# One PSUM operand for the frequent VectorE operations of four attention layers and a hybrid layer

## What is computed

```python
def rope(x, positions):                     # rotation of queries and keys
    return concatenate([x1 * cos - x2 * sin, x2 * cos + x1 * sin])
def dense_causal_attention(q, k, v, block_q):
    s = jnp.where(q_pos >= key_pos, einsum(q, k) * scale, NEG_INF)
    p = jax.nn.softmax(s, axis=-1)
    return einsum(p, v)
def rmsnorm(x, g): return x * rsqrt(mean(x * x) + eps) * g
shift, scale, gate = split(silu(c) @ ada_w[i] + ada_b[i])   # per layer, 1024 x 3072
h = rmsnorm(x, norm_g[i]) * (1 + scale) + shift
```

## Time and profile before

| | |
|---|---|
| runs, us | 3306.7, 3315.63, 3318.36 |
| profiled execution, its own time | 3318.54 us |
| its span | 3316.6 us |
| mean granted TensorE clock | 0.941 |
| TensorE busy | 3015.2 us, 91% |
| VectorE busy | 1104.9 us, 33% |
| ScalarE busy | 648.0 us, 20% |
| GpSimd busy | 883.3 us, 27% |
| stages, us from the start | MLA 113 to 387, SWA to 701, NSA to 1263, MLA to 1557, hybrid attention to 1840, the rest to 3316 |

### The profile page before, as it was taken

How to read it: one execution, slowest core, us unless ns; L and a number is a source line. 1 busy time by engine, 2 the same in 40 slices (tenths; PEclk the granted TensorE clock), 3 DMA queues, 4 the chain that set the end, 5 groups by cost and what they waited for, 6 DMA issues and landing times.

```text
span 3316.6 us, 27803 instructions
## 1 busy us (share of the span) xinstructions
PE 3015.2 (91%) x10138; PEld 1655.1 (50%) x10138; DVE 1104.9 (33%) x2086; ACT 648.0 (20%) x1460; POOL 883.3 (27%) x556
## 2 busy tenths in 40 slices
PE   1799978999999998998788978999999999999997
PEld 1356534556666654564455647444444444444443
DVE  5553365333475544534544245200000221100001
ACT  1123122321323331232133122100000100100000
POOL 4580282038180005703810000183000480000000
PEclk7799989999999998998798988999999999999999
DMA  5441342135141113412310100253222452222222
GB/s 176 138 128 46 95 133 63 40 115 143 39 127 36 29 40 113 126 57 85 111 29 1 51 25 13 84 169 114 76 65 78 134 166 76 63 76 76 68 78 69
DMA packets 267402, 278.05 MB, mean 84 GB/s; under 512 B 39093, under 2 KB 240167, under 8 KB 267175
## 3 DMA queue, kind: packets, MB, share of 16 engines
q1 hardware_dynamic: 239655, 176.04, 17.6%
q0 software_dynamic: 27648, 100.68, 9.8%
HBM read 274.59 MB, written 2.10 MB: 83 GB/s over the span
## 4 chain that ended last, share of the span: by engine, by line
PE 86%; DVE 8%; ACT 2%; DMA 2%; issue 1%; SPq 0%; DVEq 0%; PEld 0%; ACTq 0%; PEldq 0%
PE psum L673 44%; PE psum L815 10%; PE psum L1265 9%; PE psum L1100 3%; PE psum L700 3%; PE psum L789 2%; PE psum L1131 2%; PE psum L717 2%; PE psum L801 2%; PE psum L1086 2%; DVE arena L1914 1%; DVE ada_sum L1858 1%; PE psum L1136 1%; PE psum L937 1%; PE psum L938 1%
## 5 line engine op out<-in xcount | busy, mean ns | idle before, releaser
L673 PE MATMUL psum<-h,ring 128*128 128x512 f32 (+1 forms) x3216 | 1391.8, 593 | 33.0 <-ACT h L1394 29.9
L673 PEld LDWEIGHTS psum<-h,ring 128*128 128x128 f32 x3216 | 617.4, 194 | 769.7 <-issue 753.9
L600 POOL DMA_DIRECT2D ada_ring<-in_ada_w x192 | 113.1, 589 | 1836.3 <-DVE gains L1872 1600.3
L616 POOL TENSOR_TENSOR ada_sum<-ada_sum,ada_ring 128x1024 f32<-128x1024 f32 x168 | 404.2, 2406 | 13.2
L815 PE MATMUL psum<-og,ring 128*128 128x512 f32 x768 | 333.1, 593 | 2.3 <-DVE og L2377 2.0
L612 POOL TENSOR_TENSOR ada_ring<-ada_ring,cond 128x1024 f32<-128x1024 f32 x168 | 320.1, 1905 | 5.3 <-POOL ada_sum L616 1.6
L1265 PE MATMUL psum<-arena,ring 128*128 128x512 f32 x704 | 302.5, 592 | 0.0
L815 PEld LDWEIGHTS psum<-og,ring 128*128 128x128 f32 x768 | 144.6, 190 | 181.8 <-issue 178.3
L2387 DVE TENSOR_TENSOR arena<-psum,arena 128x512 f32 x44 | 30.4, 692 | 573.8 <-PE psum L673 573.8
L1265 PEld LDWEIGHTS psum<-arena,ring 128*128 128x128 f32 x704 | 133.8, 190 | 168.4 <-issue 168.4
L2010 DVE SCALAR_TENSOR_TENSOR x<-psum,mods,x 128x512 f32<-128x512 f32 x64 | 48.1, 751 | 481.3 <-PE psum L1265 272.2
(11 more groups left out here) (266 smaller groups left out, 2846.9 us busy)
## 6 DMA issues: line engine op xcount, KB each, us to landing
ada_ring<-in_ada_w POOLq DMA_DIRECT2D x192, 512.0 KB, 4.1
ring<-in_ffn_w_gate SPq DMA_DIRECT2D x22, 1024.0 KB, 5.3
ring<-in_ffn_w_up SPq DMA_DIRECT2D x22, 1024.0 KB, 5.3
ring<-in_ffn_w_down SPq DMA_DIRECT2D x32, 704.0 KB, 4.6
ring<-in_sc_w_in SPq DMA_DIRECT2D x12, 1024.0 KB, 5.1
ring<-in_mla_w_in SPq DMA_DIRECT2D x10, 1024.0 KB, 5.7
ring<-in_ada_w SPq DMA_DIRECT2D x8, 1024.0 KB, 5.5
ring<-in_mla_w_out SPq DMA_DIRECT2D x8, 1024.0 KB, 5.2
```

The costliest lines, as they stand in the source:

```text
L600: pool.dma_start(ada_ring[:, i % 2, :], w[k * P:(k + 1) * P, first(part)]).then_inc(arrived[i % 2], n.give(f"ada_in{i % 2}", 16))
L616: step = nc.gpsimd.tensor_tensor(total, total, piece, ALU.add)
L673: m = pe.matmul(tile.at[:, part], lhs(k), rhs(k), start=(k == 0), stop=(k == K - 1))
```

## The change

Every VectorE operation that is frequent in the attention layers and read two operands from SBUF, or one in the doubled rate, now reads one operand from PSUM.

- ScalarE writes the exponentials back into the score bank instead of the probs buffer. VectorE's scaling (`normalise`, `weigh`) reads the bank and writes the probs buffer; the three small operations of the compressed branch read the bank too.
- A rotation's `raw * cos` is made when the tile is taken (`take_raw`), from PSUM, beside the copy to `raw`. `rotate` multiplies the turned tile by `sin` in its own bank and adds `tmp0` to it from there. The hybrid layer keeps the old sequence under the name `rotate_normed`.
- The reciprocals of MLA's latents go to the score banks 2 and 3, and the norm reads them there.

```diff
-                        nc.scalar.activation(depth.probs(step)[:, 0:256], depth.bank(step)[:, 0:256], ACT.Exp, scale=SCALE64
+                        nc.scalar.activation(depth.bank(step)[:, 0:256], depth.bank(step)[:, 0:256], ACT.Exp, scale=SCALE64
...
-                        p, source = depth.probs(step)[:, at:at + w], depth.bank(step)
...
-                        e = nc.scalar.activation(p, source, ACT.Exp, bias=neg_max[:, step % 4, g:g + 1], scale=scale,
+                        scored = depth.bank(step) if w > T else depth.bank(step)[:, at:at + w]
+                        e = nc.scalar.activation(scored, scored, ACT.Exp, bias=neg_max[:, step % 4, g:g + 1], scale=scale,
...
+            def take_raw():
+                tile = next_tile()
                 done(tile)
                 if n.of["rope_ready"].at:
                     dve.wait_ge(S["rope_ready"], n.now("rope_ready"))
-                nc.vector.tensor_tensor(tmp[:, 0, 0:width], source, cos, ALU.mult
+                nc.vector.tensor_copy(raw[:, 0, :], tile.at)
+                nc.vector.tensor_tensor(tmp[:, 0, :], tile.at, rope[:, 0, :], ALU.mult).then_inc(tile_used[tile.bank], 1)
+                return tile
+
+            def rotate(dsts, taken):
+                tile = next_tile()
+                done(tile)
+                evacuated(taken)
+                settle(nc.vector.tensor_tensor(tile.at, tile.at, rope[:, 1, :], ALU.mult))
+                for rows_d, dst in dsts:
+                    turned = nc.vector.tensor_tensor(dst, tmp[rows_d, 0, :], tile.at[rows_d, :], ALU.add)
+                turned.then_inc(tile_used[tile.bank], 1)
+                evacuated(tile)
+                dve.sem_inc(S["rope_ready"], n.give("rope_ready"))
...
-                        last = nc.vector.tensor_scalar(p[:, at:at + w], p[:, at:at + w], row_inv[:, b, g:g + 1], None, ALU.mult)
+                            last = nc.vector.tensor_scalar(p[:, at:at + w], scored[:, at:at + w], row_inv[:, b, g:g + 1], None,
+                                                           ALU.mult)
...
-                copy_tile(raw[:, 0, :])
+                taken = [take_raw()]
...
-                    settle(nc.vector.reciprocal(lora_rms[:, i, :], lora_rms[:, i, :]))
+                    settle(nc.vector.reciprocal(SB[i], lora_rms[:, i, :]))
...
-                        last = nc.vector.scalar_tensor_tensor(lora[:, k, :], lora[:, k, :], g, lora_rms[:, i, :],
+                        last = nc.vector.scalar_tensor_tensor(lora[:, k, :], lora[:, k, :], g, SB[i],
...
-                        return nc.vector.tensor_scalar(p[:, 0:w], p[:, 0:w], row_inv[:, b, 0:1],
+                        return nc.vector.tensor_scalar(p[:, 0:w], scored[:, 0:w], row_inv[:, b, 0:1],
```

More of the change, by code:

```diff
@@ L1898, in final_norm @@
                                                    ).then_inc(S["x_normed"], n.give("x_normed"))
-            def rotate(dsts, source, tile, cos=None, sin=None, width=T):
-                cos = rope[:, 0, :] if cos is None else cos
-                sin = rope[:, 1, :] if sin is None else sin
+            def take_raw():
+                tile = next_tile()
                 done(tile)
@@ L1906, in rotate, with rotate_normed @@
                     dve.wait_ge(S["rope_ready"], n.now("rope_ready"))
-                nc.vector.tensor_tensor(tmp[:, 0, 0:width], source, cos, ALU.mult
+                nc.vector.tensor_copy(raw[:, 0, :], tile.at)
[11 more added lines that the diff above has]
+                dve.sem_inc(S["rope_ready"], n.give("rope_ready"))
+            def rotate_normed(dst, source, tile):
+                done(tile)
+                dve.wait_ge(S["rope_ready"], n.now("rope_ready"))
+                nc.vector.tensor_tensor(tmp[:, 0, :], source, C["ax_cos"], ALU.mult
                                         ).then_inc(S["dve_step"], n.give("dve_step"))
-                nc.vector.tensor_tensor(tmp[:, 1, 0:width], tile.at[:, 0:width], sin, ALU.mult
-                                        ).then_inc(tile_used[tile.bank], 1)
+                nc.vector.tensor_tensor(tmp[:, 1, :], tile.at, C["ax_sin"], ALU.mult).then_inc(tile_used[tile.bank], 1)
                 dve.wait_ge(S["dve_step"], n.now("dve_step"))
                 evacuated(tile)
-                for rows_d, dst in dsts:
-                    turned = nc.vector.tensor_tensor(dst, tmp[rows_d, 0, 0:width], tmp[rows_d, 1, 0:width], ALU.add)
-                turned.then_inc(S["rope_ready"], n.give("rope_ready"))
+                nc.vector.tensor_tensor(dst, tmp[:, 0, :], tmp[:, 1, :], ALU.add).then_inc(S["rope_ready"], n.give("rope_ready"))
             every, low, high = slice(0, P), slice(0, 64), slice(64, P)
@@ L1956, in normalise @@
                     G = len(u["groups"])
-                    p = depth.probs(done)
+                    p, scored = depth.probs(done), depth.bank(done)
                     dve.wait_ge(S["exp_done"], n.take("exp_done"))
                     if weigh is not None:
-                        weigh(u, b, p).then_inc(S["probs_ready"], n.give("probs_ready"))
+                        weigh(u, b, p, scored).then_inc(S["probs_ready"], n.give("probs_ready"))
                         return
@@ L2036, in mla @@
                     gate_tile(mla_gate[0][:, e, :], mla_sig[:, e, :], next_tile())
-                rotate([(low, mla_kpe[0:64, 0, :]), (high, mla_kpe[64:P, 1, :])], raw[:, 0, :], next_tile())
+                rotate([(low, mla_kpe[0:64, 0, :]), (high, mla_kpe[64:P, 1, :])], taken[0])
                 def part(name, pair):
@@ L2075, in query @@
                 def query(pair):
-                    copy_tile(raw[:, 0, :])
+                    taken[0] = take_raw()
                 def gate(pair):
@@ L2081, in turn @@
                 def turn(pair):
-                    rotate([(every, swa_q[:, pair % 2, :])], raw[:, 0, :], next_tile())
-                copy_tile(raw[:, 0, :])
+                    rotate([(every, swa_q[:, pair % 2, :])], taken[0])
+                taken = [take_raw()]
                 skip(1)
-                rotate([(low, swa_k[0][0:64, 0, :]), (high, swa_k[1][64:P, 1, :])], raw[:, 0, :], next_tile())
+                rotate([(low, swa_k[0][0:64, 0, :]), (high, swa_k[1][64:P, 1, :])], taken[0])
                 query(0)
@@ L2137, in turn, with weigh @@
                 def turn(pair):
-                    rotate([(every, nsa_q[:, pair % 2, :])], raw[:, 0, :], next_tile())
-                def weigh(u, b, p):
+                    rotate([(every, nsa_q[:, pair % 2, :])], taken[0])
+                def weigh(u, b, p, scored):
                     if u["branch"]:
```

25 lines of the change are left out of this document (13 added, 12 removed).

## The result

The changed kernel takes 3288.37 us, the median of five runs (3271.46, 3273.36, 3288.37, 3289.11, 3289.71); the kernel before, measured beside it, 3310.77 (3303.59 to 3318.36). The ratio of the means is 0.9914, with a 95% interval of 0.9885 to 0.9944: a gain of 28 us, where the medians are 22.4 apart. Six further runs of the changed kernel in a later comparison gave 0.9913 [0.9889, 0.9936]. The forecast was 3280 us, between 3259 and 3302. The time lies inside; the gain behind it, 35.7 us from 3315.6, came out smaller, and the kernel before measured 5 us lower beside the changed one than when the forecast was made.

What follows compares the result with a forecast made beforehand. TensorE's waits on VectorE operations, many stretched by GpSimd, bounded the possible gain at 79.8 us; terms 19.6 + 3 + 9.2 + 2.9 + 3.0 - 2 gave 35.7 us, so 3280 us, range 3259 to 3302.

Steps and rivals of the forecast that it cites:

- SWA openings, 19.6 us: Eight SWA openings: TensorE's waits on the rotation fall from 38.2 to 18.6 us, a gain between 15 and 22.6.
- The clock term of 3 us: SWA: matmuls behind long stands run at a low clock; shorter stands gain 3 us (0 to 8).
- The undisturbed opening, 2.0 us: SWA opening with GpSimd idle: TensorE's wait goes from 2.24 us to 2.0.
- MLA starts, 9.2 us: Two MLA layer starts: TensorE's wait for the rotation's addition shortens by 4.6 us each, 9.2 in all.
- the zero: MLA: copy's bank held 0.68 us longer, set against the shorter rotation behind it: zero (-2 to +1 over both layers).
- NSA, 2.9 and 3.0 us: NSA: start's wait falls from 4.9 to 2.0 us, gaining 2.9; four waits on the scaling go, gaining 3.0.
- The hybrid layer, a loss of 2 us: Hybrid attention: dearer scalings raise waits from 19.0 to 23.9 us; with some 3 back, loss 2 (gain 3 to loss 12.8).
- one collision fewer saves a stretch at lowered clock, which costs some 3: Hybrid layer: avoiding one collision keeps the clock from falling for a stretch, giving back some 3 us.
- Rival 3: Hybrid layer: idle time lowers the clock; ten more slow units cancel the gain, 18 of 32 give 3347 us; chance 0.06.
- Rival 1: SWA: the next wait, such as the sinks' addition meeting GpSimd, takes over; gain 23 us, time 3293; chance 0.14.
- some 17 and some 55: Whole kernel: stated lowest and highest total gain in us from the terms' ends, 3261 to 3299 us.
- The scaling's fixed part: PSUM scalings: by the skill page some 65 ns more each, about 2 us over the hybrid's 32 units; forecast assumed proportional cost.

Runs made afterwards that it cites:

- e5: Kernel before, with GpSimd's conditioning multiply and add narrowed from 1024 columns to 8 (all but each chunk's first multiply): 3251.45 us, ratio 0.9811.
- e6: Changed kernel with GpSimd's conditioning multiply and add narrowed from 1024 columns to 8 (all but each chunk's first multiply): 3255.55 us, ratio 0.9826.
- e4: The changed kernel run again unedited, to see how two executions differ stage by stage: 3284.52 us, ratio 0.9913.
- e1: Kernel before with only the rotations changed; exponentials, scalings and latents as before: 3287.08 us, ratio 0.9928.
- e3: Changed kernel with the hybrid layer's exponentials and scalings back in SBUF: 3280.18 us, ratio 0.9901.
- e2: Kernel before with only the exponentials and scalings moved to PSUM; rotations and latents as before: 3312.91 us, ratio 1.0009.
- e10: Changed kernel with the sinks' addition written as two one-column additions with a scalar operand: 3275.17 us, ratio 0.9888.
- e7: Changed kernel with only the first 5 units of each half of the hybrid's attention keeping exponentials in PSUM: 3274.45 us, ratio 0.9896.
- e12: Changed kernel with split sinks' addition, hybrid norms and rotations also using PSUM, and only 5 units per hybrid half in PSUM: 3268.79 us, ratio 0.9857.

## Why the prediction was right, and where not

The place and the mechanism were right. Operations with two SBUF operands stretch while GpSimd works, one operand in PSUM takes that away, and e5 and e6 show that the whole balance hangs on it. That the total fits is in part luck: the stages that can be read came out 4 us better than their terms, and the gain expected in the other two, NSA and the second MLA, can't be confirmed. By its own terms:

- **SWA openings, 19.6 us.** The waits fell by 18.1 us, in place of eight waits of 4.8 on average eight of 2.5. The term let the sinks' addition collide in three openings at 0.86 us each, 2.6 us in all; in this trace it did in three, which waited 4.8, 3.3 and 2.4 us. Without a meeting they wait 2.8, 1.9 and 1.9 (e6), so it cost some 4 us; in e4 it cost 1.7, in one opening. The clock term of 3 us: TensorE was busy for 268.8 us in place of 274.5 at a clock of 0.96 in place of 0.92, which is 5.7. In e4 the waits fell by 20.3 and the busy time by 3.6. Either way both together are near 23.8, against 22.6 in the sum.
- **The undisturbed opening, 2.0 us**, came as 1.9, in four of the eight; the first opening has 2.0, and the second 2.8 where it meets nothing.
- **MLA starts, 9.2 us.** 14.7 became 5.5: 9.2. The first stage fell by 4.2 to 4.5 us, the expected 4.6. That leaves nothing for the copy's bank, as the zero had it. The second start is in a stage that in one of eight traces was 6 us longer.
- **NSA, 2.9 and 3.0 us.** Both waits fell as said (4.9 to 2.0, and 3.0 to nothing); the stage took 562.2 before, and 558.2 to 559.4 in six of the eight traces with the new code, so it shows some 3 of these 5.9 us, against the one trace before.
- **The hybrid layer, a loss of 2 us.** The waits rose to 26.2 us (23.9 expected), but the layer came out 1.4 us shorter. By 1.4 us alone that would not be firm; the three traces with the old code there (before, e1, e3) and the four with the new (changed, e2, e4, e10) give 588.3 to 590.5 and 586.9 to 588.4. The step that failed is "one collision fewer saves a stretch at lowered clock, which costs some 3". Before, the clock was at its lower level from 1614 to 1655 us and once more from 1672 to 1679; after, only from 1571 to 1594, and that is 9.8 us of TensorE's busy time in the first half (143.2 to 133.4), while its waits for the scaling there did not fall (11.5 to 13.1). The second half's 6.3 us of loss is 16 units at 0.39, as priced.
- **Rival 3** did not happen: once the clock had risen, the second half was granted 1.00 to its end, at 9.5 to 10.3 us busy of 12. Rival 1's mechanism did, in part: the sinks' addition took some 4 us of the openings in one trace and 1.7 in the other, around the 2.6 that the forecast gave it.

**The sum.** In the stages that repeat (the first, SWA, the hybrid) I had expected 4.6 + 22.6 - 2 = 25.2 us; the traces give 4.4 + 23.7 + 1.4 = 29.5, and 1.7 more in the rest, where nothing was changed and which scatters by 3.3. In NSA and the second MLA I had expected another 10.5. The runs give 28 us altogether, with an interval of 18 to 38, so the 35.7 of the sum are not excluded, but the best value leaves nothing for those two stages. The traces say otherwise: in six and seven of eight with the new code they are 3 to 4 and 10.5 to 12 us shorter than in the one trace before. But that one is of an execution 7 us above the mean of its five, and how the kernel before scatters there isn't known. Whether those two stages gained stays open; several profiled executions of the kernel before would be needed.

Two sums in the prediction do not come out. Its terms' own ends add up to a gain of 12.3 and 51.7 us, not "some 17 and some 55", and without a collision the SWA openings would gain 22.2 and not 22.6. The measured gain lies inside either pair of ends.

**The scaling's fixed part, and short idle times.** The Trainium skill, "VectorE: DVE Perf Modes", section "The TRN2 errata", gave a PSUM scaling some 65 ns more than the width does. The widths that stand undisturbed in both kernels don't show it: 343 - 274 = 69 ns at 128 elements and 1018 - 620 = 398 at 768, which is 0.54 and 0.52 ns an element with nothing fixed on top. The Trainium skill, "TensorE: Matmul & The Clock Gate", section "A second HAM failure mode: psum-queue depth-cycling", spoke for rival 3. The traces have such falls of the clock where the units were uneven (e3, e7, and the earlier trace rows) and none for the short, even idle times: in the changed kernel's second half TensorE was busy for 9.5 us of 12 at a granted clock of 1.00.

## What to carry to other kernels

When two engines collide, test it by silencing the other engine before rewriting anything: one small edit to GpSimd here (e5, and e6 beside it) showed the size of the gain and its limit. Protect a chain from its end, the operation that TensorE waits for, since the next unprotected operation meets the collision instead, even one of two elements: e1 protects the end and has nearly all, e2 protects the start and has nothing (a part of e1's gain, up to 8 us in SWA by e5 and e6, is the operation that it moved out of the chain). Where GpSimd is idle the scaling out of PSUM only costs (5.5 to 6 us in the hybrid's second half), so choose such a form by what runs beside it, not by operation.

## What I had not expected of the hardware

- A VectorE operation of 128 x 2 elements, 0.16 us alone, took 2.15 us when it met GpSimd's 128 x 1024 multiplication and 2.25 when it met its addition. The same sum written with a scalar operand took 0.20 to 0.22 for each of its two halves, at the same places.
- ScalarE's exponential into its own PSUM bank is shorter than the one into SBUF, by the same amount at every width. After (mean ns behind the bar), where the kernel before has 363, 464, 577, 687 and 902 at 128, 256, 384, 512 and 768:

```profile
L1418 ACT ACTIVATE psum<-psum,neg_max 128x256 f32<-128x256 f32 x96 | 42.1, 439 | 6.4 <-DVE neg_max L1961 6.4
L1418 ACT ACTIVATE psum<-psum,neg_max 128x512 f32<-128x512 f32 x48 | 31.8, 662 | 10.7 <-DVE neg_max L1961 10.7
L1418 ACT ACTIVATE psum<-psum,neg_max 128x768 f32<-128x768 f32 x32 | 28.0, 875 | 86.5 <-DVE neg_max L1947 86.5
```

- Waits of nearly the same total can go with a different clock: in the hybrid's first half, scalings of 1.02 us each, 16.3 us in all, went with a granted clock that stayed at 1.00 once it had risen, and scalings between 0.62 and 2.5 us, 18.5 in all (e3), with two more falls to the lower level. Every trace with uneven scalings behind the first rise has such a fall (before, e1, e3, e7, e12) and none with even ones has. That evenness and not the single long wait is the cause was not tested apart.
